# First expert stage: the tokens' rows selected by stationary one-hot products instead of fetched from DRAM

## The reference, cut to what matters

```python
f = hier_moe(jnp.concatenate([hl2, hc2], axis=0), *moe_args)   # 512 tokens x 1024
# in it: each token chooses 2 of 32 experts (first a group of 8, then the best 2 in it),
# with gates; then for each expert e, over the rows xblk of the tokens that chose it:
(jax.nn.silu(xblk @ w1[e]) * (xblk @ w3[e])) @ w2[e]           # w1, w3: 1024x512, w2: 512x1024
# and each result, times its gate, is added to its token's row
```

## Time and profile before

| | |
|---|---|
| median of 3 runs | 2095.07 us |
| profiled execution, its own time | 2096.56 us |
| its span | 2094.8 us |
| TensorE busy | 1892.8 us (90%), mean granted clock 0.955 |
| VectorE busy | 978.7 us (47%) |
| ScalarE busy | 316.2 us (15%) |
| DMA | 607.30 MB, 290 GB/s over the span |
| first expert stage, groups 0 to 15 | about 1024.5 to 1480.0 us |
| attention between the stages | to about 1654 us |
| second expert stage | to the end |

### The profile page before, as it was taken

One profiled execution on the slowest core, in us unless ns is written; L12 is line 12 of the kernel. 1 busy time (PEld: TensorE's weight loads), 2 busy tenths in 40 slices (PEclk: granted clock), 3 DMA queues, 4 the chain that ended last, 5 costly groups with the idle time before them and its releaser, 6 DMA issues.

```text
span 2094.8 us, 22927 instructions
## 1 busy us (share of the span) xinstructions
PE 1892.8 (90%) x9459; PEld 1050.5 (50%) x9459; DVE 978.7 (47%) x1793; ACT 316.2 (15%) x718; POOL 30.8 (1%) x45
## 2 busy tenths in 40 slices
PE   8999999999999999999999998999999966556567
PEld 5758874555588845884633333333456522122222
DVE  5538888466378895646522322322565410111111
ACT  2221110226211103011300000000235200000000
POOL 0000000000000000000100000000000000000000
PEclk9999999999999999999999999999999987787779
DMA  8458886451278864421899999999821899999998
GB/s 324 153 194 276 283 284 222 148 186 42 82 268 294 285 234 168 136 110 71 319 424 427 426 427 427 426 427 425 297 92 75 325 427 426 426 426 426 427 426 337
DMA packets 148602, 607.30 MB, mean 290 GB/s; under 512 B 14312, under 2 KB 65192, under 8 KB 124049
## 3 DMA queue, kind: packets, MB, share of 16 engines
q1 hardware_dynamic: 144224, 595.90, 72.7%
q0 software_dynamic: 4176, 9.81, 1.3%
q10 hardware_dynamic: 96, 0.10, 0.0%
HBM read 606.46 MB, written 3.28 MB: 291 GB/s over the span
## 4 chain that ended last, share of the span: by engine, by line
PE 78%; DMA 15%; DVE 2%; issue 2%; ACT 1%; SPq 1%; DVEq 0%
PE psum L2848 15%; PE psum L1185 15%; PE psum L552 9%; PE psum L2883 7%; DMA ring<-in_w 6%; PE psum L1125 6%; PE psum L2001 4%; DMA arena<-in_w 4%; PE psum L2943 4%; DMA consts<-in_w 3%; PE psum L2088 2%; PE psum L612 2%; DMA normed_t<-in_w 1%; PE psum L691 1%; PE psum L1475 1%
## 5 line engine op out<-in xcount | busy, mean ns | idle before, releaser
L1185 PE MATMUL psum<-normed_t,ring 128*128 128x256 f32 x1408 | 306.4, 380 | 0.0
L1185 PEld LDWEIGHTS psum<-normed_t,ring 128*128 128x128 f32 x1408 | 266.9, 190 | 43.5 <-issue 7.2
L2848 PE MATMUL psum<-ring,arena 128*32 128x512 f32 (+1 forms) x752 | 234.3, 667 | 56.9 <-DMA normed_t<-in_w 17.8
L1037 DVE SCALAR_TENSOR_TENSOR arena<-ring,silu_c,arena 128x1024 f32<-128x1024 f32 x168 | 204.7, 1279 | 0.0
L552 PE MATMUL psum<-ring,normed_t 128*128 128x512 f32 x448 | 198.1, 599 | 3.6 <-DVE resid L3341 1.5
L2848 PE MATMUL psum<-consts,arena 128*32 128x512 f32 (+1 forms) x288 | 147.0, 668 | 23.6 <-DMA ring<-in_w 19.0
L3341 DVE TENSOR_TENSOR resid<-resid,psum 128x512 f32<-128x512 f32 x128 | 79.6, 682 | 178.1 <-PE psum L2943 178.1
L2848 PE MATMUL psum<-arena 128*32 128x512 f32 (+1 forms) x300 | 114.4, 668 | 32.2 <-DMA arena<-in_w 19.7
L552 PEld LDWEIGHTS psum<-ring,normed_t 128*128 128x128 f32 x448 | 84.5, 192 | 106.3 <-issue 105.3
L2848 PEld LDWEIGHTS psum<-ring,arena 128*32 128x32 f32 (+1 forms) x752 | 64.2, 131 | 146.4 <-issue 146.4
L3356 DVE TENSOR_TENSOR scaled<-scaled,psum 128x512 f32<-128x512 f32 x24 | 16.5, 688 | 202.1 <-PE psum L2848 202.1
(11 more groups left out here) (613 smaller groups left out, 2876.4 us busy)
## 6 DMA issues: line engine op xcount, KB each, us to landing
ring<-in_w SPq DMA_DIRECT2D x90, 2048.0 KB, 32.2
arena<-in_w SPq DMA_DIRECT2D x36, 2048.0 KB, 31.7
consts<-in_w SPq DMA_DIRECT2D x26, 2048.0 KB, 33.3
ring<-in_w_mod SPq DMA_DIRECT2D x24, 2048.0 KB, 7.9
ring<-in_ffn_w_up SPq DMA_DIRECT2D x44, 1024.0 KB, 7.7
normed_t<-in_w SPq DMA_DIRECT2D x18, 2048.0 KB, 30.7
ring<-in_ffn_w_down SPq DMA_DIRECT2D x10, 2048.0 KB, 7.8
ring<-in_ab_w_in SPq DMA_DIRECT2D x6, 2048.0 KB, 15.7
```

The source lines that it names most:

```text
L1037: ins = dv.scalar_tensor_tensor(out=acc, in0=w, scalar=sc, in1=acc, op0=ALU.mult, op1=ALU.add)
L1185: m = pe.matmul(PS[:, b, 256 * hf:256 * hf + 256], w[:, hf, k, P * cc:P * cc + P], HT[:, k, 0:T], start=(k == 0), stop=(k == KC - 1))
L2848: m = pe.matmul(PS[r, 2 + q, :], self.XT[c % 2][k // 4][:, k % 4, r], self.weights(c, q, h, FE * k, FE), start=k == 0, stop=k == KC - 1)
```

## The change

Only the first expert stage changes.

- The copy of the rows to DRAM and the 15 indirect fetches on GpSimd go away. The rows of every group are made on TensorE by `pe_first`: one-hot matrices `SEL` (128 tokens by 32 slots) are the stationary side, and the token rows `XM` the moving side. Each quarter of the slots sums over two token tiles: 2 halves of the columns, 2 tiles, 4 quarters, 16 calls with 512 columns each, into banks 6 and 7. ScalarE copies both banks to `FIRST_ROWS` (`rows0`, `rows1`), and `pe_turn` transposes that as before. VectorE makes `SEL` for each group (`sel`). Group 0 goes the same way instead of by `pe_select`.
- `pe_first(c+1)` stands behind `pe_hidden(c, 1)`, where `pe_turn(c+1)` was; `pe_turn(c+1)` now stands behind `hidt`.
- The spreads of the group before come earlier: the first ahead of `pe_hidden(c, 0)`, the second between the two hidden products. All 8 adds on VectorE follow one another. Banks of the second spread change to 6, 5, 7, 4.
- `XT` has one buffer instead of two.
- The 12 tiles of the last two groups are loaded in halves, the first halves of a pair ahead of the second ones, and their products wait for each half.

The diff, cut to its core (12 leading spaces are left out):

```diff
     four = lambda v: v.rearrange("p (j r) -> p j r", j=4)
-    self.XT = [[four(v[:, 0:512]), four(v[:, 512:1024])] for v in (self.turned, Z[:, 3072:4096])]
+    self.XT = [[four(v[:, 0:512]), four(v[:, 512:1024])] for v in [self.turned] * 2]
...
     self.CT = R[:, 400:400 + 32 * (nt + self.halves)].rearrange("p (t e) -> p t e", e=NE)
-    first_at = R[:, 592:600] if nt == 4 else DEAD[:, 3520:3584]
+    first_at = PRM[:, 306:434] if nt == 4 else DEAD[:, 3520:3584]
...
     one_hot = lambda v: v.rearrange("p (t h r) -> p t h r", t=nt, h=self.lanes)
-    self.SEL = [one_hot(XSF[:, 1280:1280 + P * nt])] + ([one_hot(SM[:, 256:512])] * (self.groups - 1) if nt == 2 else [])
+    later = SM[:, 256:512] if nt == 2 else XSF[:, 512:768]
+    self.SEL = [one_hot(XSF[:, 1280:1536])] + [one_hot(later)] * (self.groups - 1)
+    self.on_chip = range(self.groups)
...
         pe.wait_ge(self.w_loaded[i], 16 * (len(self.slots[i]) * (turn + 1) + more))
+def second_half(self, c, q):
+    i = 3 * (c - self.groups) + q + self.halved
+    return self.second_halves[i] if i >= 0 else None
+def load_halves(self, sp, c, q):
+    for half in range(2):
+        for h in range(self.lanes):
+            n = self.tile(c, q, h)
+            if half == 0:
+                sp.wait_ge(sems["pe"], upto("pe", self.done_with(n - self.ns)))
+            cols = slice(2048 * half, 2048 * half + 2048)
+            sp.dma_start(self.slots[n % self.ns][0][:, cols], self.source(n)[:, cols])\
+                .then_inc(self.second_half(c, q) if half else self.w_loaded[n % self.ns], 16)
...
 def pe_turn(self, te, c):
-    pe, p, L, b = te.eng, te.p, self.L, c % 2
+    pe, p, L = te.eng, te.p, self.L
...
         pe.wait_ge(sems["dve"], upto("dve", f"{L}.sel.{c}"))
-    else:
-        pe.wait_ge(self.rows_in[b], 16 * (c // 2) + 16 * b)
...
+def pe_first(self, te, c):
+    pe, p, L = te.eng, te.p, self.L
+    pe.wait_ge(sems["dve"], upto("dve", f"{L}.sel.{c}"))
+    if c >= 2:
+        pe.wait_ge(sems["dve"], upto("dve", f"{L}.add13.{c - 2}"))
+    for hf in range(2):
+        if c == 0:
+            wait(pe, *te.banks[6 + hf])
+        for j in range(2):
+            for q in range(4):
+                t = 2 * (q % 2) + j
+                m = pe.matmul(PS[ROOM * q:ROOM * q + ROOM, 6 + hf, :], self.SEL[c][:, t, q // 2, :], XM[:, t, 512 * hf:512 * hf + 512],
+                              start=j == 0, stop=j == 1)
+        p.step(m, f"{L}.first{hf}.{c}")
...
         wait(pe, *(("act", f"{L}.silu.{c - 1}") if q == 0 else ("dve", f"{L}.prod.{c - 1}")))
-    if c >= 2 and q == 0 and self.nt == 4:
-        pe.wait_ge(sems["dve"], upto("dve", f"{L}.add13.{c - 2}"))
...
             pe.wait_ge(sems["dve"], upto("dve", f"{L}.xt1.{c}"))
+        if k == 4 and self.second_half(c, q):
+            pe.wait_ge(self.second_half(c, q), 16 * self.lanes)
...
     p.step(m, f"{L}.hidt.{c}")
-    if c >= 1 and not ending:
-        if self.nt == 4:
-            self.pe_spread(te, c - 1, 1)
-        else:
-            self.pe_combine(te, c - 1, (2, 3))
+    if self.nt == 4 and c + 1 in self.on_chip:
+        self.pe_turn(te, c + 1)
+    if c >= 1 and not ending and self.nt == 2:
+        self.pe_combine(te, c - 1, (2, 3))
...
         product(1, (2, 3))
-    elif last:
+    elif self.second_half(c, 2):
...
             product(n, (0, 1))
-        pe.wait_ge(self.last_parts[0], 16 * self.lanes)
+        pe.wait_ge(self.second_half(c, 2), 16 * self.lanes)
...
         return ((4, 6, 5, 0), (3, 7, 1, 2))[n][t]
-    return ((5, 0, 4, 1), (5, 3, 2, 0))[n][t]
+    return ((5, 0, 4, 1), (6, 5, 7, 4))[n][t]
...
     pe.wait_ge(sems["dve"], upto("dve", f"{L}.yx{n}.{c}"))
-    if n == 1 and c < self.groups - 1:
+    if n == 0 and c < self.groups - 1:
+        pe.wait_ge(sems["act"], upto("act", f"{L}.xt0.{c + 1}"))
+        pe.wait_ge(sems["dve"], upto("dve", f"{L}.xt1.{c + 1}"))
+    elif c < self.groups - 1:
+        pe.wait_ge(sems["dve"], upto("dve", f"{L}.add02.{c}"))
         pe.wait_ge(sems["dve"], upto("dve", f"{L}.add00.{c}"))
-        if c + 2 < self.groups:
-            pe.wait_ge(sems["act"], upto("act", f"{L}.xt0.{c + 2}"))
...
     for c in range(self.groups):
+        if c >= 1 and self.nt == 4:
+            self.pe_spread(te, c - 1, 0)
...
         elif c >= 1:
-            self.pe_spread(te, c - 1, 0)
+            self.pe_spread(te, c - 1, 1)
...
         self.pe_hidden(te, c, 1)
-        if c + 1 < self.groups:
+        if self.nt == 4 and c + 1 in self.on_chip:
+            self.pe_first(te, c + 1)
+        elif c + 1 < self.groups:
...
     p.step(ac.activation(self.g0, self.g0, ACT.Exp), f"{L}.dexp")
+    def rows_of(c):
+        for hf in range(2):
+            ac.wait_ge(sems["pe"], upto("pe", f"{L}.first{hf}.{c}"))
+            p.step(ac.activation(FIRST_ROWS[:, 512 * hf:512 * hf + 512], PS[:, 6 + hf, :], ACT.Copy), f"{L}.rows{hf}.{c}")
+    if self.nt == 4:
+        rows_of(0)
...
         p.step(ac.activation(HS, PS[:, 2, :], ACT.Silu), f"{L}.silu.{c}")
-        if c + 1 < self.groups:
+        made = self.nt == 4 and c + 1 in self.on_chip
+        if made:
+            rows_of(c + 1)
+        elif c + 1 < self.groups:
...
         p.step(ac.activation(self.HGT, PS[:, 4, :].rearrange("p (j r) -> p j r", j=4), ACT.Copy), f"{L}.hgt.{c}")
+        if made:
+            self.act_xt(ac, p, c + 1)
...
         if nt == 4:
+            if hot.shape[3] == ROOM:
+                every = [P, nt * n, ROOM]
+                return dv.tensor_tensor(hot.rearrange("p t n r -> p (t n) r"), numbers.rearrange("p t n -> p (t n)").unsqueeze(2).to_broadcast(every),
+                                        cst("number_in_slot")[:, 0:ROOM].unsqueeze(1).to_broadcast(every), ALU.is_equal)
...
     for c in range(self.groups):
-        if nt == 2 and c + 1 < self.groups:
-            if c >= 1:
+        if c + 1 in self.on_chip:
+            if nt == 2 and c >= 1:
                 dv.wait_ge(sems["pe"], upto("pe", f"{L}.turn1.{c}"))
+            elif c >= 1:
+                dv.wait_ge(sems["pe"], upto("pe", f"{L}.first1.{c}"))
...
         if nt == 4 and c:
-            for t in (0, 2, 1, 3):
-                add_spread(c - 1, 0, t)
+            for n in range(2):
+                for t in (0, 2, 1, 3):
+                    add_spread(c - 1, n, t)
...
             dv.wait_ge(gate_loaded[1 + 2 * l], 64 - 48 * l)
-        elif nt == 4:
-            for t in (0, 2, 1, 3):
-                add_spread(c - 1, 1, t)
-        else:
+        elif nt == 2:
...
-def pool(self, po):
-    L = self.L
-    if self.nt == 2:
-        return
-    for t in range(self.nt):
-        po.wait_ge(sems["act"], upto("act", f"{L}.xm{t}0"))
-        po.wait_ge(sems["act"], upto("act", f"{L}.xm{t}1"))
-        po.dma_start(xm_dram[P * t:P * t + P, :], XM[:, t, :]).then_inc(self.xm_written, 16)
-    po.wait_ge(sems["dve"], upto("dve", f"{L}.list"))
-    po.wait_ge(self.xm_written, 16 * self.nt)
-    for c in range(1, self.groups):
-        po.wait_ge(sems["pe"], upto("pe", f"{L}.turn1.{max(c - 2, 0)}"))
-        po.indirect_dma_start(XG[:, c % 2, :], None, xm_dram[:, :], bass.IndirectOffsetOnAxis(ap=LIST[:, c:c + 1], axis=0),
-                              bounds_check=4 * P - 1, oob_is_err=False).then_inc(self.rows_in[c % 2], 16)
```

More of the change, by code:

```diff
@@ L2573, in build_program @@
         XM = Z[:, 0:4096].rearrange("p (t n) -> p t n", t=4)
-        XG = Z[:, 0:2048].rearrange("p (b n) -> p b n", b=2)
+        FIRST_ROWS = CST[:, AB_DEAD + 1024:AB_DEAD + 2048]
         XSF = XS.rearrange("p t d -> p (t d)")
@@ L2602, in __init__ @@
                 self.over_row_made = s("over_row_made")
-                self.last_parts = [s(f"last_part{i}_loaded") for i in range(1 if nt == 4 else 2)]
-                self.rows_in = [s(f"rows_in{b}") for b in range(2)]
+                self.last_parts = [s(f"last_part{i}_loaded") for i in range(2)] if nt == 2 else []
+                self.halved = 6 if nt == 4 else 0
+                self.second_halves = [s(f"second_half{i}_loaded") for i in range(self.halved)]
                 self.units = [(t, n) for g in range(nt // 2) for n in range(2) for t in (2 * g, 2 * g + 1)]
@@ L2733, in load_weights @@
                 src = self.source(n)
-                if n >= self.tiles - self.lanes:
+                if n >= self.tiles - self.lanes and self.nt == 2:
                     view, of = self.last_part(n, 0)
@@ L2746, in last_part @@
                 slot, src = self.slots[n % self.ns][0], self.source(n)
-                if self.lanes == 2:
-                    return slot[:, 2048 * i:2048 * i + 2048], src[:, 2048 * i:2048 * i + 2048]
                 rows, cols = (slice(0, 4), slice(0, 2), slice(2, 4))[i], slice(512 * (i > 0), 512 * (i > 0) + 512)
@@ L2770, in sp @@
                             self.load_early(sp, n, part)
-                for n in range(self.ns + 4, self.tiles):
+                for n in range(self.ns + 4, self.tiles - self.lanes * self.halved):
                     self.load_weights(sp, n)
```

(19 more changed lines are left out.)

1 line of the change is left out of this document (removed).

## The result

The changed kernel takes 2125.64 us (median of 4 runs, 2125.12 to 2130.08) against 2095.56 us: ratio 1.0142, 95% interval 1.0127 to 1.0157, 30.1 us slower. The forecast was 2123.4 us, in a range of 2116 to 2131, and slower. The profiled execution took 2125.94 us, with a span of 2124.1 us.

The account below looks back on a forecast made before the run. TensorE was taken to become the first expert stage's bound: 1050.1 + 14 x 30.85 + 26.3 = 1508.3 us, 28.3 later than before. Added to 2096.56, less 1.49 to the median, this gives 2123.4 us, range 2116 to 2131.

Parts of the forecast that it names:

- What bounds the stage: First expert stage: TensorE at 27.17 us a group, weights 29.6; with the change TensorE becomes the bound at 30.85.
- The price of `pe_first`: TensorE, each group: 32 instructions in 8 rounds of 0.43, 3.44 us, plus 0.15 for a change of shape.
- The other change of shape: TensorE, spread right behind the `w2` product: 0.09 us a group.
- the 30.85: Forecast period of a group in us: 27.17 before plus 3.68 of added TensorE work.
- The covers: ScalarE copies `rows1` and `hgt` hidden behind `hidt` and the turn, 0.2 us to spare; failure costs 0.1 to 0.6 a group.
- Group 0: Selection 2.4 us sooner, second hidden product to `w2` product 2.55 us more; group 1 starts 0.15 us later, at 1050.1.
- The rest of the program: Attention and second expert stages move one to one with the last `w2` product's end, 28.3 us later.
- The cover of 23.5 us: DMA waits in groups 8 to 15, the only cover for TensorE's added work of 55 us; it is used up.
- The rivals: Transfers stay bound, 3%; half price, 3%; TensorE and ScalarE alternate, 6%; quarters not side by side, 3%; rows still fetched, under 1%.

Follow-up runs that it names:

- The halved calls: Changed kernel with 8 instead of 16 calls of `pe_first` in groups 1 to 15; 2101.36 us, ratio 1.0026.
- the bytes given back: Changed kernel with the row copy to DRAM and 15 indirect fetches issued again into a buffer nobody reads; 2127.81 us, ratio 1.0148.
- with all fetched: Changed kernel in its own order, only group 0 by `pe_first`, groups 1 to 15 fetched by GpSimd again; 2091.62 us, ratio 0.9978.
- with the spreads back: Changed kernel with the spreads in their places of before, all rows selected on the chip; 2127.25 us, ratio 1.0156.

## Why the prediction was right

- **What bounds the stage.** Right: TensorE was at its own pace in the early groups and waited only from group 8 on, so its added work showed. The halved calls confirm the slope (24.3 us for 25.8), the bytes given back confirm that they no longer counted.
- **The price of `pe_first`.** 3.44 + 0.15 us against 3.57 measured, read from products of the same form in the other stage. The other change of shape was put at 0.09 and comes to 0.22: the first hidden product, now behind a spread, takes 7.02 us where it took 6.87, and the `w2` product, now behind the turn, 7.09 where it took 7.02. This is the whole 0.13 us by which the period of 30.98 is over the 30.85, 1.8 us over 14 groups.
- **The covers.** For groups 1 to 14 right: no wait for `hgt` or `rows1`. For the last group wrong: I took only the turn away from it (26.3 us), and it also loses what covered `prod` (0.8 us) and the spread that covered `hgt` (0.9 us). It took 28.28 us (1481.87 to 1510.15), 2.0 us more. The first of the two was there to be read before: in the last group of the kernel before, which has no turn behind its hidden product either, TensorE waits for `prod` from 1469.15 to 1469.91:

```profile
1469.17 0.70 DVE scaled L3356
1469.91 0.75 PE psum L2865 x4
```
- **Group 0.** From the start of the first selection to the first spread of group 1: 33.0 us forecast (1017.1 to 1050.1), 33.1 measured (1015.02 to 1048.10). That it began 2.1 us sooner comes from ahead of the stage, where the code is the same: over all the profiled executions of the changed orders the first selection begins anywhere from 1012.3 to 1019.1. So the stage grew by 32.2 us, 3.9 over the forecast's 28.3 (1.8 + 2.0 and rounding), and 2.1 of it are offset by the earlier start, 0.8 by what follows the stage. That the time came out within 2.3 us of the forecast is in this part luck; without these two it would have been about 2128.5, still in the range.
- **The rest of the program.** As forecast it moved along: 614.0 us from the last `w2` product's end to the span's end, 614.8 before.
- **The cover of 23.5 us.** The sum was right but for the 0.8 us of `prod` in the last group, which are in the 23.5 and are no wait for weights. A claim under it was not right: that waits late in the stage are a reserve that extra work in any group may use in full. The runs with groups 0 to 3 and 0 to 5 on the chip in the order of before refute it (4.9 and 5.6 us of 10.6 and 18.6 were not covered). In the changed kernel this made no difference, because all groups carried the work and TensorE bound the stage throughout.
- **The rivals.** None occurred. The cover of `hgt` did fail, but in the orders of the experiments: by 0.86 us a group with all fetched, and through `xt0` with the spreads back.

## What to carry to other kernels

Where two resources of a stage take nearly the same time (27.2 us of TensorE; 29.6 us of weights, and 30.1 with the fetched rows, as measured from group 8's `w2` product to group 15's), moving work from the slower to the faster one pays only up to the gap: here 3.8 us were added to save 0.5. Waits at the end of a stage are only a partial reserve for its beginning when the slots ahead are few: extra work early in the stage starves the transfers of slots, even though nobody waits yet. And when an instruction is moved, look at what it stood in front of: the spread covered `hgt`, the turn covered `prod`, and each cost 0.86 us a group where it was left bare.

## What was not expected of the hardware

Four column quarters of TensorE ran side by side at one round of 0.43 us whether neighbouring calls were for different quarters or for the same one (3.57 against 3.61 us for 32 instructions), so up to four instructions in a row for one quarter did not hold up the others. How many it takes to do so was not tried. The product behind one of another shape took 0.15 us longer behind a spread (7.02 against 6.87 us) and 0.22 longer behind a transpose (7.09).
